# Turning residual rows and feed-forward values by transposing DMAs instead of identity matmuls

## The reference

```python
# first block
x = x + concat([ya, yb]) @ w_out            # attention heads, then a residual
h = rmsnorm(x, norm_ffn)
x = x + (silu(h @ w_gate) * (h @ w_up)) @ w_down     # width 5632
x = rmsnorm(x, norm_final)
# second block
merged = g_a * (a_out @ w_proj_a) + g_m * (m_out @ w_proj_m)
x = x + merged @ w_out
h2 = rmsnorm(x, norm2_g)
u = causal_dwconv(h2 @ w_up, conv_w, conv_b)         # 3 taps along the sequence, 2 x 5632 columns
u_gate, u_val = split(u)
x = x + (silu(u_gate) * u_val) @ w_down
```

## Time and profile before

| | us |
|---|---|
| median of 3 runs | 2542.74 |
| lowest, highest | 2542.72, 2543.06 |
| the profiled execution, its own time | 2542.45 |
| its span, first to last instruction | 2540.7 |
| TensorE busy | 2533.9 |
| VectorE busy | 1413.6 |
| ScalarE busy | 1229.0 |
| GpSimd busy | 138.8 |

### The profile page before, as it was taken

How to read it: one execution, slowest core, us unless ns; L and a number is a source line. 1 busy time by engine, 2 the same in 40 slices (tenths; PEclk the granted TensorE clock), 3 DMA queues, 4 the chain that set the end, 5 groups by cost and what they waited for, 6 DMA issues and landing times.

```text
span 2540.7 us, 33424 instructions
## 1 busy us (share of the span) xinstructions
PE 2533.9 (100%) x11596; PEld 2099.3 (83%) x11596; DVE 1413.6 (56%) x1707; ACT 1229.0 (48%) x1698; POOL 138.8 (5%) x211
## 2 busy tenths in 40 slices
PE   9999999999999999999999999999999999999999
PEld 7888888888888888888888888888888888888887
DVE  5555555555555555555455555565566646665665
ACT  6555445444344434455444544544555445553553
POOL 2222200000000000000000111100000000000000
PEclk9999999999999999999999999999999999999999
DMA  8555556665666566666666666655666566666665
GB/s 239 161 171 161 169 173 185 191 189 189 193 190 189 190 192 190 191 198 190 179 185 179 182 185 179 184 176 189 184 182 190 190 192 187 178 193 195 184 189 166
DMA packets 327827, 471.16 MB, mean 185 GB/s; under 512 B 23232, under 2 KB 126244, under 8 KB 327584
## 3 DMA queue, kind: packets, MB, share of 16 engines
q1 hardware_dynamic: 326352, 467.30, 61.3%
q0 software_dynamic: 1088, 2.07, 0.3%
q10 hardware_dynamic: 272, 0.26, 0.0%
HBM read 467.44 MB, written 2.11 MB: 185 GB/s over the span
## 4 chain that ended last, share of the span: by engine, by line
PE 99%; DMA 0%; SPq 0%; DVE 0%; ACT 0%; issue 0%
PE ps L473 32%; PE ps L475 32%; PE ps L474 31%; PE ps L922 1%; PE ps L722 1%; PE ps L567 0%; PE ps L549 0%; PE ps L582 0%; PE ps L555 0%; PE ps L756 0%; PE ps L639 0%; PE ps L659 0%; PE ps L888 0%; DMA raw<-in_w_in 0%; PE ps L592 0%; PE ps L863 0%
## 5 line engine op out<-in xcount | busy, mean ns | idle before, releaser
L1395 DVE TENSOR_TENSOR w_lo<-raw,w_hi 128x1024 fp32r<-128x1024 f32 x880 | 1081.1, 1230 | 1078.6 <-ACT w_hi L976 1076.5
L976 ACT ACTIVATE w_hi<-raw 128x1024 fp32r<-128x1024 f32 x880 | 931.3, 1060 | 1182.3 <-PE ps L475 1172.9
L473 PE MATMUL ps<-w_hi,xT_hi 128*128 128x512 f32 x2204 | 873.3, 396 | 0.5 <-DVE xT_lo L1414 0.5
L475 PE MATMUL ps<-w_hi,xT_lo 128*128 128x512 f32 x2204 | 859.8, 390 | 0.0
L474 PE MATMUL ps<-w_lo,xT_hi 128*128 128x512 f32 x2204 | 858.3, 389 | 0.0
L473 PE MATMUL ps<-w_hi,yT_hi 128*128 128x512 f32 x1312 | 515.2, 393 | 0.0
L475 PE MATMUL ps<-w_hi,yT_lo 128*128 128x512 f32 x1312 | 511.2, 390 | 0.0
L474 PE MATMUL ps<-w_lo,yT_hi 128*128 128x512 f32 x1312 | 510.6, 389 | 0.0
L475 PEld LDWEIGHTS ps<-w_hi,xT_lo 128*128 128x128 f32 x2204 | 413.7, 188 | 87.2
L473 PEld LDWEIGHTS ps<-w_hi,xT_hi 128*128 128x128 f32 x2204 | 414.0, 188 | 85.9 <-issue 2.7
L474 PEld LDWEIGHTS ps<-w_lo,xT_hi 128*128 128x128 f32 x2204 | 414.2, 188 | 82.9
(11 more groups left out here) (204 smaller groups left out, 899.7 us busy)
## 6 DMA issues: line engine op xcount, KB each, us to landing
raw<-in_w_up SPq DMA_DIRECT2D x264, 512.0 KB, 3.7
raw<-in_w_down SPq DMA_DIRECT2D x176, 512.0 KB, 3.8
raw<-in_w_in SPq DMA_DIRECT2D x160, 512.0 KB, 3.8
raw<-in_w_gate SPq DMA_DIRECT2D x88, 512.0 KB, 3.7
raw<-in_w_out SPq DMA_DIRECT2D x60, 512.0 KB, 3.7
raw<-in_w_in SPq DMA_DIRECT2D x128, 192.0 KB, 2.8
raw<-in_w_in SPq DMA_DIRECT2D x192, 128.0 KB, 2.5
raw<-in_w_proj_m SPq DMA_DIRECT2D x16, 512.0 KB, 3.8
```

The source lines that it names most:

```text
L473: pe.matmul(o, hi[:, q], w_hi[n % NS][:, k, 0:width], start=first, stop=False)
L475: mm = pe.matmul(o, lo[:, q], w_hi[n % NS][:, k, 0:width], start=False, stop=last)
L976: nc.scalar.activation(w_hi[n % NS][:, :, 0:width], raw[n % NS][:, :, 0:width], ACT.Copy).then_inc(hi_ready, 1)
L1395: v.tensor_tensor(w_lo[n % NS][:, :, 0:width], raw[n % NS][:, :, 0:width], f32(w_hi[n % NS][:, :, 0:width]), ALU.subtract).then_inc(lo_rea ...
```

## The change

All 49 turns go by DMA. Per turn: GpSimd splits each of the two token tiles into its low and its high 16-bit halves (`halve`, one copy of 1024 16-bit elements each); ScalarE waits for each and issues a transposing DMA (`send_across`; 256 KB, eight blocks of 128x128 16-bit elements) from its queue; GpSimd waits for both (`landed`) and for the readers of the last turn, and joins the halves (`join`, two copies of 1024 16-bit elements) into `turned` in SBUF. The readers on ScalarE and VectorE read `turned` in place of PSUM; each turn has the same `turned`, where before the turns alternated between two pairs of banks or parts of them. TensorE's `turn_x`, `turn_act` and `turn_u` are gone. `halves`, `flipped` and `turned` lie in one tile `work` with `stage`, `prob`, `mix`, `pT` and `y`, whose users are the attention heads. ScalarE's loops in both feed-forwards become unrolled code, as do GpSimd's copies of x. The lines of the new kernel are other ones: `send_across` L947, `x_hi` L1077, `first_tap` L1288, `split` on ScalarE L914, `halve` L1944, `join` L1949.

```diff
+        halves = work[:, 0:4 * S].bitcast(U16).rearrange("p (t e n) -> p t e n", t=NT, e=2)
+        flipped = work[:, 4 * S:8 * S].bitcast(U16).rearrange("p (e f s) -> p e f s", e=2, s=S)
+        turned = work[:, 8 * S:12 * S].rearrange("p (f s) -> p f s", s=S)
+        turned_halves = work[:, 8 * S:12 * S].bitcast(U16).rearrange("p (n e) -> p n e", e=2)
...
-            def turn_x(q, base, summed=None):
...
-            def turn_act(up, fg, i):
...
-            def turn_u(g, fg, i):
...
+            def send_across(i, k, step=0):
+
+                for t in range(NT):
+                    act.wait_ge(halved, at(i, 2 * k + t + 1, 2 * step))
+                    act.dma_start_transpose(flipped[:, :, :, t * P:(t + 1) * P].rearrange("p e f s -> p (e f) s"),
+                                            halves[:, t, :, :].rearrange("p e n -> p (e n)")).then_inc(across, 16)
...
@@ ScalarE, residual: behind(u)
+                            if u == done(early and i == 0, units, g):
+                                send_across(0, TURNS[name] + 2 * i + g)
@@ ScalarE, ffn1: behind(u)
+                            if u == 0:
+                                send_across(i, TURNS["ffn1"] + fg0 - 1, 1)
@@ ScalarE, ffn2: scaled(i, g)
                         evac(up, i, g, tok_u[g], 0, W, rstd)
+                        send_across(i, TURNS["ffn2"] + 2 * fg0 + g, 2)
...
+            def halve(z, t):
+
+                g_.tensor_copy(halves[:, t, :, :], z[:, t, :].bitcast(U16).rearrange("p (n e) -> p e n", e=2)).then_inc(halved, 1)
+
+            def join(b):
+
+                c = slice(b * 2 * S, (b + 1) * 2 * S)
+                return g_.tensor_copy(turned_halves[:, c, :], flipped.rearrange("p e f s -> p (f s) e")[:, c, :])
+
+            def landed(i, k, step=0):
+                pool.wait_ge(across, at(i, 32 * (k + 1), 32 * step))
+
+            def turn_x(name, base, kept=True):
...
+                            halve(fresh[g], t)
+                        if kept:
+                            g_.tensor_copy(x[:, :, (2 * i + g) * W:(2 * i + g + 1) * W], fresh[g]).then_inc(x_kept, 1)
+                        landed(i, TURNS[name] + g, 2)
+                        pool.wait_ge(kt_lo, at(i, base + 4 * g, 8))
+                        for b in range(2):
+                            join(b).then_inc(kt_T, 1)
...
@@ GpSimd, second feed-forward
+                        for tt in range(NT):
+                            pool.wait_ge(by_act, at(i, FREE + PH[f"ffn2_up{t}"][BY_ACT] + 2 * g + tt + 1, 4))
+                            halve(tok_u[g], tt)
+                        landed(i, TURNS["ffn2"] + 2 * fg0 + g, 2)
+                        pool.wait_ge(conv_step, at(i, 16 * fg0 + 8 * g, 16))
+                        join(0)
+                        join(1).then_inc(tok_u_T[g], 1)
```

More of the change, by code:

```diff
@@ L25 @@
 X = mybir.AxisListType.X
+U16 = mybir.dt.uint16
 P = 128
@@ L136, in evacuated @@
     return FREE + PH[name][1] + 2 * (3 * (head // 4) + groups[head % 4])
+TURNS, turns_ = {}, 0
+for name_, n_ in (("out_a", 4), ("ffn1", 11), ("ffn1_down2", 4), ("proj_a", 4), ("out2", 4), ("ffn2", 22),):
+    TURNS[name_], turns_ = turns_, turns_ + n_
 def at(i, c, step):
@@ L709, in _, with residual @@
                           behind=lambda u: heads(96 + 8 * i + u), also=(by_act, FREE + PH["out_b"][BY_ACT]) if g else None)
-            def turn_x(q, base, summed=None):
[L715 to L726, removed]
-                for i in range(2):
[L730 to L738, removed]
+            def residual(name, units, src, kt0, ready=None, also=None, behind=nothing, early=False):
+                for i in range(2):
+                    if i == 1:
+                        behind = nothing
                     if early and i == 0:
@@ L744, in residual @@
                               ready=ready, behind=behind, also=also if g else None)
-            residual("out_a", 4, yT, 0, KT, ready=lambda u: pe.wait_ge(ha.y_lo, FREE + UK * (u + 1)))
-            def turn_act(up, fg, i):
[L752 to L758, removed]
+            residual("out_a", 4, yT, 0, ready=lambda u: pe.wait_ge(ha.y_lo, FREE + UK * (u + 1)))
             def ffn1():
@@ L787, in ffn1 @@
                     if t == 2:
[L788 removed]
+                        residual(down, units, yT, 0, ready=act_ready, early=True)
                     else:
@@ L791, in ffn1 @@
                             for g in range(2):
-                                group(down, i, 2 * units, g, units, yT, 0, evac_free(by_dve, down, BY_DVE, i, g), ready=act_ready,
-                                      behind=first if i == 0 else nothing)
+                                group(down, i, 2 * units, g, units, yT, 0, evac_free(by_dve, down, BY_DVE, i, g), ready=act_ready)
                     fg0 += n_fg
@@ L961, in ffn2 @@
                             group(down, i, 2 * units, g, units, xT, 0, evac_free(by_dve, down, BY_DVE, i, g), ready=act_ready,
-                                  behind=first if i == 0 else nothing, halves=t == 2 and i == 1 and g == 1)
+                                  halves=t == 2 and i == 1 and g == 1)
                     fg0 += n_fg
@@ L1371, in ffn2 @@
                     turn(up, 0, 16, behind)
-                    with act.Fori(1, n_fg) as i:
+                    for i in range(1, n_fg):
                         def behind(u):
@@ L2002, in _ @@
             g_.tensor_tensor(half_r_sq[:], rstd[:], half_r[:], ALU.mult).then_inc(ffn_scale, 1)
-            keep("ffn1_down2")
+            fg0 = 0
+            for t, width in enumerate(THIRDS):
+                for i in range(width // W):
+                    for tt in range(NT):
+                        pool.wait_ge(by_dve, at(i, FREE + PH[f"ffn1_up{t}"][BY_DVE] + 3 + tt, 4))
+                        halve(tok_act, tt)
+                    landed(i, TURNS["ffn1"] + fg0, 1)
+                    pool.wait_ge(tok_lo, at(i, FREE + 2 * fg0, 2))
+                    join(0)
+                    join(1).then_inc(tok_T, 1)
+                fg0 += width // W
+            turn_x("ffn1_down2", 2 * KT)
             pool.wait_ge(ss_ready, 2)
```

105 lines of the change are left out of this document (43 added, 62 removed).

## The result

The change makes the kernel slower: 2634.15 us (median of 4 runs, 2632.91 to 2635.53) against 2542.74, a ratio of 1.036 with a 95% interval of 1.035 to 1.037. The forecast was 2600, from 2515 to 2760. The profiled execution of after spans 2633.7 us where before spans 2540.7, so 93.0 us have to be explained.

What follows compares the result with a forecast made beforehand. TensorE, busy 2533.9 of 2540.7 us, was taken as the bound. 2542.45 - 43 (transposes) + 44 (second feed-forward) + 56 (residual rows) + 0 (first feed-forward) = 2599.5, said as 2600 us, range 2515 to 2760.

Steps and rivals of the forecast that it cites:

- Gain, 43 us: On TensorE: removing 392 transposes in 49 turns saves 0.88 us a turn, 43 us, all on the path.
- Prices of the parts: Per turn, on GpSimd and ScalarE: each halve 1.04 us, each join 1.6, each issue of a transposing DMA 1.5.
- Landing: Transposing DMAs: each lands 4.0 us from the start of its issue, 2.5 behind its end; raw loads left at 3.7.
- Second feed-forward, +44: 22 turns: TensorE waits 0.8 us per gate turn, 2.7 per up turn, 0.5 for late loads; 4.0 times 11.
- Residual rows, +56: 16 turns: TensorE waits 36 us in out_a and proj_a together, 15 in ffn1_down2, 5 in out2.
- First feed-forward, 0: 11 turns: joins end near 15 us, what stands behind is due at 19.0, so no waits.
- The clock, 1.00: TensorE's granted clock, 1.00 (2.4 GHz) before the change; the sum had no term for a fall.
- rival 3: Slow transposing DMA, 3.7 us per issue, makes ScalarE the bound: 2790 us, clock could fall to 1.2 GHz; chance 0.2.
- signs of being wrong: Issues under 0.5 or over 3 us, raw loads landing much later than 3.7, clock below 1.00, waits starting in ffn1.
- Rival 1: Transfers stay hidden, 2521 us; decided below about 1.0 us per issue together with 1.3 per join; chance 0.15.
- rival 2: Gain and waits cancel with issues of 1.0 us and joins of 1.3: 2545 us; chance 0.07.

Runs made afterwards that it cites:

- e12: The change with residual rows and each third's last up turn on TensorE, second feed-forward readers two units later, SyncE issuing there: 2519.49 us, ratio 0.991.
- e11: The change with each raw load in the second feed-forward's up stages cut to 128 of 512 columns (values wrong): 2590.67 us, ratio 1.019.
- e10: As e9, but the gate's two transposing DMAs are sent one unit later, behind the w_hi of unit 8: 2556.37 us, ratio 1.005.
- e1: The change with only the first feed-forward's 11 turns by DMA, residual rows and second feed-forward back on TensorE: 2534.93 us, ratio 0.997.
- e8: The kernel before the change with ten pauses of TensorE put into the first feed-forward, no transposing DMA: 2609.53 us in one run.
- e4: The change with each transposing DMA replaced by a plain copy of the same 256 KB (values in wrong order): 2593.51 us, ratio 1.020.
- e9: The change with residual rows and second feed-forward up turns on TensorE, gate readers there two units later: 2526.83 us, ratio 0.994.

## Why the prediction was right, and where not

The direction and its reason hold: the transposes' gain is paid for several times over by waits that start in ScalarE's queue. The time came out 34 us above the likeliest value, inside the range. By the steps:

- **Gain, 43 us.** Right: 0.88 a turn in every stage where nothing waits (the stages of e12; the first feed-forward's up1 went from 176.8 to 174.1 with three turns).
- **Prices of the parts.** Halve: 1.04 taken, median 1.04, but 1.33 on average beside w_lo. Join: 1.6 taken; undisturbed 1.15 to 1.22, on average 1.47. So the step of 2 KB adds a tenth to a fifth to the 1.04. The rule of the Trainium skill that I weighed (GPSIMD Engine Reference, "Performance pitfalls for Q7 kernels"), half as much again, is not borne out by these rows, which are plain copies. The issue, 1.5 taken, is 1.30 where the stream is quiet and 1.64 in the second feed-forward.
- **Landing.** Mis-sized. I took 2.5 us behind the end of an issue wherever it falls, and argued that 10 GB/s of transfers on 186 of loads disturb nothing. Landing is 3.6 us from the issue in proj_a and out2, 5.7 in the second feed-forward, 3.3 there with light loads (e11), and 8.3 in e10. It is longest where a load is issued among the sends (e10, and 7 pairs of the change). The loads suffer too, 4.5 us where I had left them at 3.7.
- **Second feed-forward, +44.** The three terms, against TensorE's waits in the trace: gate turns 0.8 forecast and 1.3 measured (11 turns, 14.6 us); up turns 2.7 and 3.7 (the 8 inside up stages, 29.5). The step that failed is the last up turn of each third. I let its readers feed only the splits, but the down stage's own unit 6 needs its product: TensorE waits there 7.9 and 4.9 us for xT_lo (L1808), and 4.1 in the last one, where the trace names w_lo. In all 61.7 us of waits instead of 44.
- **Residual rows, +56.** Oversized as waits, 28 us; with the clock the cost is 44. Turns follow at 14.6 to 16.5 us in out_a and 15.6 to 15.8 in proj_a, near the forecast's 16.4, but TensorE waited only 8.6 us for the four turns of out_a where I had charged every delay in full, 17.8. That this term was too large hides part of what the others lack: that the sum was only 34 us short owes something to luck.
- **First feed-forward, 0.** Right: about 1 us, and e1 is faster than before.
- **The clock, 1.00.** The largest miss: about 34 us of the ledger's 47. It stood only in rival 3 ("could fall to 1.2 GHz") and among the signs of being wrong, and should have been a term of the sum, since the forecast itself had waits of 5.5 us. e8 shows that such waits are enough. The rest of the 47, what a pause itself adds to the matmul records, was not in the sum either.
- **Rivals.** Rival 1 did not occur, and its deciding point was wrong: e4 has issues of 0.60 and joins of 1.21 on average, both below what I named, and still loses 51 us. The readers' place and the landing decide. Rival 3's prices did not occur: the median issue is a third of 3.7, and a whole transfer lands in 5.3 us (median). The Trainium skill (VectorE: DVE Perf Modes, "The three transpose paths") gives 1309 ns a block, from which I had estimated 10.5 us for eight in a row; the trace doesn't agree, its median being half of that. Two sums of the rivals were also off: rival 1's waits add up to 24 and not 22, and rival 2 names 30 for the residual rows and adds 35. Neither is large enough to matter here.

The sum with measured terms: -43 for the transposes, +89 of idle time (61.7 in the second feed-forward, 27.9 in the residual stages), +47 of longer matmuls, about 34 of them the clock: +93.

What stays open: the residual stages with their readers later were not tried, nor was the port between GpSimd and VectorE taken away, so its share of the late halves and joins is not known. That a load issued among the sends delays them is shown by moving the send (e9, e10) and by sorting the pairs of the change; its price apart from the other effects of the move is not known. e8 rests on one run; its reading is of the clock column and not of its time.

## What to carry to other kernels

A transfer that replaces work on the critical engine is hidden only if two queues agree: the one that issues it must have nothing urgent behind the issue, and the readers must stand later than issue, landing under load and unpacking together; moving the issue to the queue with slack and the readers two units back turned a loss of 3.6% into a gain of 0.9%, with the three turns whose result is needed at once, and the residual rows, left on TensorE. Price a landing with the load that can get in among the sends, and look at what your own wait holds back: a send placed one unit later let a load go first and cost 30 us. Where a sum holds waits of TensorE of about 2 us and more, it needs a term for the clock.

## What the runs showed of the hardware that I had not expected

- TensorE's own idle time brings its clock to 1.2 GHz: not after 1.1 us, 3.4 us at 0.50 after 2.1, up to 10.2 after 12.2 (e8). Waits around 2 us go either way: in the change 1.79 was followed by a fall and 2.83 was not. There the clock cost 34 us on top of 89 us of waits.
- A transposing DMA of 128 x 1024 elements of 16 bits lands no later than a plain copy of the same size (5.3 us both, e4), and differs in the issue: 1.30 against 0.60 us on the queue that issues it.
- Two issues back to back from one queue: in proj_a the second took 1.35 us like the first, in the second feed-forward up to 3.8. Light loads bring the median to 1.25 (e11), so a busy DMA side reaches back into the engine that issues.
- A transfer of 256 KB lands in 3.3 us beside light loads (e11) and in 5.1 beside full ones that are issued before or behind both sends (e9, e12); with one load of 512 KB issued among them the median is 8.3 (e10).
